# One GELU and one diagonal per expert slot, and a ring of seven buffers, in a decoder trunk with 16,384 gathered experts

## The chip, the cores and the metric

The kernel runs on one core of one Trainium2 chip. The metric is the device time of one execution in microseconds; a median of several runs is compared. The profile is of one execution, and its own time is given beside its span.

## The reference

The input x has 512 rows of 1024 float32 values. There are two layers. Each is a mixer with a residual, then an expert stage with a residual; a final RMS norm ends it. The first mixer is gated linear attention beside dilated attention, the second a gated linear recurrence. The expert stage is the same in both layers:

```
s = einsum(q, sub_keys)                       # 8 heads, two lists of 128 scores each
top_s, top_i = top_k(s, 16)
cand_s = top_s[..., 0, :, None] + top_s[..., 1, None, :]
best_s, best_c = top_k(cand_s, 16)            # 16 experts per head: 8 * 16 = 128 slots per row
g = softmax(best_s)
u, v = u_tab[ids], v_tab[ids]                 # one row of 1024 of each table per slot
act = gelu(einsum('nkd,nd->nk', u, x)) * g
out = einsum('nk,nkd->nd', act, v)
```

Every row of x thus gathers 128 expert rows of u and of v in each layer.

## The kernel before

The 512 rows are four tiles of 128 (one row per partition). With two layers that makes 8 passes, p = 0 to 7, of 128 slots, k = 0 to 127, so n = 128 p + k counts 1024 slots. Tables u and v are stored side by side, so one slot's gather brings 128 rows of 2048 float32 (8 KB each, 1 MB together) into one buffer of a ring. A slot goes through five hands:

- GpSimd (`pool`, L270) issues the gather of slot n into buffer n % BUFS once slot n - BUFS is summed (`v_done`).
- VectorE (`dot`, L287) waits until it has landed and multiplies the u half with the row of x, summing along the row: one value per partition in `hid`.
- ScalarE (`activate`, L292) applies GELU to two slots at once, pair m = slots 2m and 2m + 1, when both are dotted.
- VectorE (`place`, L302) writes for each of the two slots a 128 x 128 diagonal holding GELU value times gate. There are DIAGS = 4 diagonals; slot n reuses that of slot n - 4, so it waits for `v_done` of that slot.
- TensorE (`sum_rows`, L319) multiplies the diagonal with the v half and accumulates over the 128 slots of a pass in PSUM. The last matmul signals `v_done`, which frees the ring buffer.

The order in which VectorE does this is written by hand. In the main loop it runs `dot` of slot k, and at even k it then places the pair of slots k - 2 and k - 1. So slot 2m is placed after the dot of slot 2m + 2, two slots later. At the start of a pass the last pair of the pass before is placed after dot 0, and its sum is added to the residual (`add`, L308) after dot 2. The first ten slots (EARLY = 10) are dotted and partly placed between the steps of the first tile's choice.

Everything else is woven between the slots at fixed k. VectorE does the choice of experts for the next passes (`head`: the top 16 of two lists; `candidates`, `greatest`, `places`, `picked`, `numbers`, `gates` at the offsets STEPS behind PAIR_AT) and its part of the mixers. ScalarE does exponentials, evictions and norms. TensorE does projections in pieces, up to three behind one slot. SyncE loads the projection weights, 88 blocks of 1 MB, into two buffers. The gathers and the weights use the same 16 DMA engines.

The choice keeps its scratch in a shared region of SBUF: `topf`, `posi`, `posf`, `idf` for all heads, and `spare` (L152 to L160 write and read it in `greatest`) as a tile of its own. Each step of the choice ends in `link`, which makes VectorE wait for its own last instruction.

Of the kernel before, what the change touches and what calls it, by code (L numbers as in the profile page):

```python
# [10 lines left out]
U32 = mybir.dt.uint32  # L11
ALU = mybir.AluOpType
ACT = mybir.ActivationFunctionType
AX = mybir.AxisListType

P = 128
# [3 lines left out]
NT = T // P  # L20
# [16 lines left out]
PH, PK, NKEYS = 8, 16, 128  # L37
HK = PH * PK
# [12 lines left out]
NCAND = _at  # L51
# [33 lines left out]
ROOM = 48312  # L85


BUFS = 6
DIAGS = 4
HALF = T // 2  # L90


# [18 lines left out]
class Choice:  # L111
# [5 lines left out]
    def __init__(self, nc, s, consts, scores, room):  # L117
        self.nc, self.iota, self.scores = nc, consts["iota"], scores
        self.work = room.sb("work", [P, 2, NKEYS])
        self.cv, self.ci, self.spare = (room.sb(f"cand_{x}", [P, 2, NCAND]) for x in ("sum", "id", "left"))  # L120
        self.at = room.sb("cand_at", [P, NCAND])
        self.pick = [room.sb(f"pick{k}", [P, PK, NCAND]) for k in range(2)]
        self.top = room.sb("top", [P, 2 * PH, PK])
        self.topi = room.sb("topi", [P, 2 * PH, PK], U32)
        self.topf = room.sb("topf", [P, 2 * PH, PK])
        self.best = room.sb("best", [P, PH, PK])
        self.posi = room.sb("posi", [P, PH, PK], U32)
        self.posf = room.sb("posf", [P, PH, PK])
        self.idf = room.sb("idf", [P, HK])
        self.idi = room.sb("idi", [P, 2, HK], I32)  # L130
        self.gate = room.sb("gate", [P, 2, HK])
        self.den = room.sb("den", [P, PH])
        self.tick = room.sb("tick", [P, 1])
        self.links = 0
        self.chain, self.diff, self.exped, self.chosen, self.gated = (
            s.sem(f"choice_{x}") for x in ("chain", "diff", "exped", "chosen", "gated"))
# [31 lines left out]

    def candidates(self, dve, g):
        nc, halves = self.nc, slice(4 * g, 4 * g + 4)  # L170
        self.link(dve, nc.vector.tensor_copy(self.topf[:, halves], self.topi[:, halves]))
        tf = self.topf[:, halves].rearrange("p (h o) k -> p h o k", o=2)
        tv = self.top[:, halves].rearrange("p (h o) k -> p h o k", o=2)
        self.link(dve, nc.vector.tensor_scalar(tf[:, :, 0], tf[:, :, 0], float(NKEYS), None, ALU.mult))
        for src, dst in ((tv, self.cv), (tf, self.ci)):
            for a0, na, nb, at in CAND:
                out = dst[:, :, at:at + na * nb].rearrange("p h (a b) -> p h a b", a=na)
                one = src[:, :, 0, a0:a0 + na].unsqueeze(3).to_broadcast([P, 2, na, nb])
                two = src[:, :, 1, 0:nb].unsqueeze(2).to_broadcast([P, 2, na, nb])
                last = nc.vector.tensor_tensor(out, one, two, ALU.add)  # L180
        self.link(dve, last)

    def greatest(self, dve, g):
        heads = slice(2 * g, 2 * g + 2)
        self.best_of(dve, [(self.cv[:, k], self.spare[:, k], self.best[:, 2 * g + k], self.posi[:, 2 * g + k]) for k in range(2)])
        self.link(dve, self.nc.vector.tensor_copy(self.posf[:, heads], self.posi[:, heads]))

    def places(self, dve, g):
        at = self.at[:].unsqueeze(1).to_broadcast([P, PK, NCAND])
        for k in range(2):  # L190
            pos = self.posf[:, 2 * g + k].unsqueeze(2).to_broadcast([P, PK, NCAND])
# [3 lines left out]
    def picked(self, dve, g):  # L195
        for k in range(2):
            ids = self.ci[:, k].unsqueeze(1).to_broadcast([P, PK, NCAND])
            last = self.nc.vector.tensor_tensor(self.pick[k][:], self.pick[k][:], ids, ALU.mult)  # L198
        self.link(dve, last)

    def numbers(self, dve, p, g):

        nc = self.nc
        for k in range(2):
            h = 2 * g + k
            last = nc.vector.tensor_reduce(self.idf[:, h * PK:(h + 1) * PK], self.pick[k][:], AX.X, ALU.add)  # L206
        self.link(dve, last)
        slots, heads = slice(2 * g * PK, (2 * g + 2) * PK), slice(2 * g, 2 * g + 2)
        nc.vector.tensor_copy(self.idi[:, p % 2, slots], self.idf[:, slots]).then_inc(self.chosen, 1)
# [19 lines left out]
    def step(self, dve, p, g, at):  # L229

        if at == self.STEPS[0]:
            self.candidates(dve, g)
        if at == self.STEPS[1]:
            self.greatest(dve, g)
        if at == self.STEPS[2]:
            self.places(dve, g)
        if at == self.STEPS[3]:
            self.picked(dve, g)
        if at == self.STEPS[4]:
            self.numbers(dve, p, g)  # L240
        if at == self.STEPS[5]:
            self.gates(dve, p, g)


class Experts:
# [41 lines left out]
        self.nc.vector.tensor_tensor_reduce(out=row, in0=row, in1=self.ps[:, 6:8], scale=1.0, scalar=0.0, op0=ALU.mult, op1=ALU.add,  # L287
                                            accum_out=self.hid[:, k:k + 1]).then_inc(self.dotted, 1)

    def activate(self, act, p, m):  # L290
        act.wait_ge(self.dotted, p * HK + 2 * m + 2)
        self.nc.scalar.activation(self.act_out[:, 2 * m:2 * m + 2], self.hid[:, 2 * m:2 * m + 2], ACT.Gelu_apprx_tanh).then_inc(self.gelued, 1)  # L292

    def place(self, dve, p, m):
        dve.wait_ge(self.gelued, p * HK // 2 + m + 1)
        if m % PK == 0:
            dve.wait_ge(self.choice.gated, p * self.choice.PAIRS + m // PK + 1)
        for k in (2 * m, 2 * m + 1):
            n = p * HK + k
            if n >= DIAGS:  # L300
                dve.wait_ge(self.v_done, n - DIAGS + 1)
            self.nc.vector.tensor_scalar(self.diagonal[:, n % DIAGS], self.ident[:], self.act_out[:, k:k + 1],  # L302
                                         self.choice.gate[:, p % 2, k:k + 1], ALU.mult, ALU.mult).then_inc(self.placed, 1)

    def add(self, dve, p):
        dve.wait_ge(self.v_done, (p + 1) * HK)
# [877 lines left out]
EARLY = 10  # L1184
# [20 lines left out]
def trunk(nc, A, out):  # L1205


    with Scope(nc, "main") as s:
# [6 lines left out]
        room = Room(nc, s, ROOM)  # L1215
# [76 lines left out]
        def _(act):  # L1292
# [35 lines left out]
            for i in range(PH):  # L1328
                tail0.act_q(act, 0, i)
                if i:  # L1330
                    tail0.act_scores(act, 0, i - 1)
                if i == 3:
                    choice.exponentials(act, 0, 0)
                if i in (4, 5, 6):
                    experts.activate(act, 0, i - 4)
# [4 lines left out]
            experts.activate(act, 0, 3)  # L1340
            mix0.in_act(act, 1, 0)
            experts.activate(act, 0, 4)
# [80 lines left out]
        def _(dve):  # L1423
# [25 lines left out]
            for i in range(PH):  # L1449
                tail0.rank_dve(dve, 0, i)  # L1450
                if i % 2:
                    choice.candidates(dve, i // 2)
                    choice.greatest(dve, i // 2)
                    choice.places(dve, i // 2)
                    choice.picked(dve, i // 2)
# [86 lines left out]
            experts.place(dve, 2 * NT - 1, HK // 2 - 1)  # L1542
            experts.add(dve, 2 * NT - 1)
            final.mean_dve(dve, NT - 1)
            final.dve(dve, NT - 1)
# [170 lines left out]
```

## Time and profile before

| | |
|---|---|
| median of 3 runs | 3393.06 us (3392.06 to 3418.19) |
| the profiled execution | 3395.63 us, span 3393.8 us |
| TensorE matmul busy | 2763.0 us (81%) |
| VectorE busy | 2162.3 us (64%) |
| GpSimd busy | 983.5 us (29%) |
| ScalarE busy | 536.0 us (16%) |
| moved | 1182.28 MB, mean 348 GB/s |
| mean granted TensorE clock | 0.951 of full speed |

Times in rows are microseconds from the start of the span. "DMA share" is the mean busy share of the 16 DMA engines in a stretch; PEclk is the granted clock, 1.00 being 2.4 GHz.

### The profile page before, as it was taken

The page shows a single profiled execution, that of the slowest core. Times are in us where ns is not written, and L with a number is a line of the kernel's source. Part 1 is how long each engine was busy: PE and PEld are TensorE (multiplying, and loading weights), DVE is VectorE, ACT ScalarE, POOL GpSimd, SP SyncE. Part 2 cuts the span into 40 slices and gives each one's busy share as a digit, 9 for nine tenths or more (in the row PEclk, how much of TensorE's full clock was granted, in tenths as well). Part 3 has the DMA queues.
Part 4 walks back from the last instruction along what each step waited for, and adds up shares of the span by engine and source line. Part 5 has one row for each costly group of instructions (what it writes and reads, how often), then busy time and mean ns, then how long its engine had stood idle before and what let it go on. Part 6 is the DMA issues. An engine that isn't in the chain of part 4 may idle for free.

```text
span 3393.8 us, 33961 instructions
## 1 busy us (share of the span) xinstructions
PE 2763.0 (81%) x11992; PEld 2268.8 (67%) x11992; DVE 2162.3 (64%) x6642; ACT 536.0 (16%) x1181; POOL 983.5 (29%) x1028
## 2 busy tenths in 40 slices
PE   8989988888986877888887878878987767667776
PEld 6777776677775766767775766766776555555555
DVE  1257666675776766576677667576677656567444
ACT  3122105301111124001011105101111000001000
POOL 0002333333332233332333333332333333333332
PEclk9999999999999999999999999999999998988889
DMA  5357999999999999999999999999999999999998
GB/s 175 103 211 295 381 386 370 358 371 369 391 352 374 361 377 361 384 371 360 379 377 353 373 374 357 384 370 364 388 382 337 365 349 356 361 337 364 351 357 306
DMA packets 166634, 1182.28 MB, mean 348 GB/s; under 512 B 19376, under 2 KB 19904, under 8 KB 23872
## 3 DMA queue, kind: packets, MB, share of 16 engines
q0 software_dynamic: 147456, 1073.81, 82.5%
q1 hardware_dynamic: 19008, 106.31, 8.1%
q8 instruction: 94, 1.54, 0.2%
q14 instruction: 76, 0.62, 0.1%
HBM read 1177.95 MB, written 2.10 MB: 348 GB/s over the span
## 4 chain that ended last, share of the span: by engine, by line
DMA 44%; PE 38%; issue 9%; DVE 9%; ACT 1%; POOL 0%; SPq 0%; DVEq 0%; ACTq 0%; POOLq 0%
DMA main_ring<-in_uv,main_idi 43%; PE main_bank L319 26%; PE main_bank L355 5%; PE main_bank L353 4%; DVE main_ring L287 2%; DVE main_diagonal L302 2%; DVE main_topi L160 1%; DVE main_work L152 1%; DVE main_topi L154 0%; DVE main_hid L287 0%; PE main_bank L715 0%; DVE main_top L149 0%; DVE main_top L157 0%; DVE main_pick L198 0%; DVE main_idf L206 0%
## 5 line engine op out<-in xcount | busy, mean ns | idle before, releaser
L319 PE MATMUL main_bank<-main_ring,main_diagonal 128*128 128x256 f32 (+1 forms) x8160 | 2062.7, 404 | 596.5 <-DVE main_diagonal L302 594.4
L319 PEld LDWEIGHTS main_bank<-main_ring,main_diagonal 128*128 128x128 f32 x8160 | 1608.6, 201 | 970.1 <-DVE main_diagonal L302 711.4
L287 DVE CUSTOM_DVE_ANT_0 main_ring<-main_ring,main_bank 128x1024 f32<-128x1024 f32 x1024 | 1247.6, 1220 | 1013.6 <-DMA main_ring<-in_uv,main_idi 1003.6
L270 POOL DMA_INDIRECT main_ring<-in_uv,main_idi x1024 | 983.3, 960 | 2387.3 <-PE main_bank L319 2142.8
L292 ACT ACTIVATE main_act_out<-main_hid 128x2 f32<-128x2 f32 x512 | 104.1, 203 | 2596.0 <-DVE main_hid L287 2583.1
L355 PE MATMUL main_bank<-main_xT,main_w_block 128*128 128x256 f32 x1408 | 358.8, 384 | 4.5 <-ACT main_xT L388 4.5
L302 DVE TENSOR_SCALAR main_diagonal<-main_ident,main_act_out,main_gate 128x128 f32<-128x128 f32 x1024 | 308.8, 347 | 2.4 <-ACT main_act_out L292 2.1
L355 PEld LDWEIGHTS main_bank<-main_xT,main_w_block 128*128 128x128 f32 x1408 | 270.1, 192 | 42.5 <-ACT main_xT L388 5.0
L355 PE MATMUL main_bank<-main_xT_query,main_w_block 128*128 128x256 f32 x512 | 123.9, 383 | 0.9 <-ACT main_xT_query L388 0.9
L355 PEld LDWEIGHTS main_bank<-main_xT_query,main_w_block 128*128 128x128 f32 x512 | 98.3, 193 | 14.8 <-ACT main_xT_query L388 1.2
L292 ACT ACT_TABLE_LOAD x80 | 102.6, 1283 | 1.4
L353 PE MATMUL main_bank<-main_w_block,main_xT 128*128 128x256 f32 x384 | 93.5, 382 | 0.0
L287 DVE DVE_READ_ACCUMULATOR2_ANT main_hid<- 128x1 f32 x1024 | 84.8, 83 | 0.0
L353 PEld LDWEIGHTS main_bank<-main_w_block,main_xT 128*128 128x128 f32 x384 | 72.4, 191 | 10.5 <-issue 0.9
L353 PE MATMUL main_bank<-main_w_block,main_a_gate 128*128 128x256 f32 x256 | 67.4, 387 | 0.0
L353 PE MATMUL main_bank<-main_w_block,main_mixT 128*128 128x256 f32 x256 | 62.8, 387 | 0.7 <-ACT main_mixT L826 0.7
L198 DVE TENSOR_TENSOR main_pick<-main_pick,main_cand_id 128x800 f32<-128x800 f32 x64 | 60.5, 986 | 0.6
L192 DVE TENSOR_TENSOR main_pick<-main_posf,main_cand_at 128x800 f32<-128x800 f32 x64 | 60.4, 986 | 0.2
L206 DVE TENSOR_REDUCE main_idf<-main_pick 128x16 f32<-128x800 f32 x64 | 60.0, 979 | 0.2
L353 PEld LDWEIGHTS main_bank<-main_w_block,main_a_gate 128*128 128x128 f32 x256 | 50.2, 196 | 7.4
L353 PEld LDWEIGHTS main_bank<-main_w_block,main_mixT 128*128 128x128 f32 x256 | 49.6, 195 | 7.9 <-ACT main_mixT L826 0.9
L143 DVE MEMSET main_tick<- 128x1 f32 x704 | 41.5, 59 | 2.2
(188 smaller groups left out, 1183.5 us busy)
## 6 DMA issues: line engine op xcount, KB each, us to landing
main_w_block<-in_w_query SPq DMA_DIRECT2D x32, 1024.0 KB
main_w_block<-in_w_ab SPq DMA_DIRECT2D x24, 1024.0 KB
main_ring<-in_uv,main_idi POOLq DMA_INDIRECT x1024
main_w_block<-in_w_c_in SPq DMA_DIRECT2D x16, 1024.0 KB
main_w_block<-in_w_out SPq DMA_DIRECT2D x8, 1024.0 KB
main_w_block<-in_w_c_out SPq DMA_DIRECT2D x8, 1024.0 KB
main_att_bias<-in_att_bias SPq DMA_DIRECT2D x16, 256.0 KB
main_resid<-in_x SPq DMA_DIRECT2D x2, 1024.0 KB, 7.6
```

Source lines behind the costliest of these rows:

```text
L143: self.nc.vector.memset(self.tick[:], 0.0)
L152: last = nc.vector.match_replace(copy, best[:, low], values, NEG)
L192: last = self.nc.vector.tensor_tensor(self.pick[k][:], pos, at, ALU.is_equal)
L198: last = self.nc.vector.tensor_tensor(self.pick[k][:], self.pick[k][:], ids, ALU.mult)
L206: last = nc.vector.tensor_reduce(self.idf[:, h * PK:(h + 1) * PK], self.pick[k][:], AX.X, ALU.add)
L270: nc.gpsimd.indirect_dma_start(self.ring[n % self.bufs], None, self.uv[p // NT], bass.IndirectOffsetOnAxis(self.choice.idi[:, p % 2, k:k + ...
L287: self.nc.vector.tensor_tensor_reduce(out=row, in0=row, in1=self.ps[:, 6:8], scale=1.0, scalar=0.0, op0=ALU.mult, op1=ALU.add, accum_out=s ...
L292: self.nc.scalar.activation(self.act_out[:, 2 * m:2 * m + 2], self.hid[:, 2 * m:2 * m + 2], ACT.Gelu_apprx_tanh).then_inc(self.gelued, 1)
L302: self.nc.vector.tensor_scalar(self.diagonal[:, n % DIAGS], self.ident[:], self.act_out[:, k:k + 1], self.choice.gate[:, p % 2, k:k + 1], ...
L319: last = self.nc.tensor.matmul(self.ps[:, 4 + at // T, at % T:at % T + wide], self.diagonal[:, n % DIAGS], self.ring[n % self.bufs][:, D + ...
L353: last = nc.tensor.matmul(out, xT[:, d, cols], w[:, d], start=d == 0, stop=d == KD - 1)
L355: last = nc.tensor.matmul(out, w[:, d, cols], xT[:, d], start=d == 0, stop=d == KD - 1)
```

## The change

GELU and diagonal are made for each slot by itself: `activate` and `place` take a slot k and not a pair. Slot k is activated as soon as it is dotted and placed right behind the dot of slot k + 1, whether k is even or odd. The residual add moves from behind dot 2 to behind dot 1 of the next pass. The ring has seven buffers in place of six, and three diagonals in place of four. To make room in SBUF, the scratch of the choice is kept for one pair of heads (`topf`, `posi`, `posf`, `idf`), and `topf` and `spare` lie on top of the `pick` tiles, which are written after they are read.

```diff
-BUFS = 6
-DIAGS = 4
+BUFS = 7
+DIAGS = 3
...
-        self.cv, self.ci, self.spare = (room.sb(f"cand_{x}", [P, 2, NCAND]) for x in ("sum", "id", "left"))
+        self.cv, self.ci = (room.sb(f"cand_{x}", [P, 2, NCAND]) for x in ("sum", "id"))
         self.at = room.sb("cand_at", [P, NCAND])
+        at_pick = room.next
         self.pick = [room.sb(f"pick{k}", [P, PK, NCAND]) for k in range(2)]
+        self.topf = room.part("topf", at_pick, [P, 4, PK])
+        self.spare = room.part("cand_left", at_pick + PK * NCAND, [P, 2, NCAND])
...
-        self.posi = room.sb("posi", [P, PH, PK], U32)
-        self.posf = room.sb("posf", [P, PH, PK])
-        self.idf = room.sb("idf", [P, HK])
+        self.posi = room.sb("posi", [P, 2, PK], U32)
+        self.posf = room.sb("posf", [P, 2, PK])
+        self.idf = room.sb("idf", [P, 2 * PK])
...
-    def activate(self, act, p, m):
-        act.wait_ge(self.dotted, p * HK + 2 * m + 2)
-        self.nc.scalar.activation(self.act_out[:, 2 * m:2 * m + 2], self.hid[:, 2 * m:2 * m + 2], ...)
-
-    def place(self, dve, p, m):
-        dve.wait_ge(self.gelued, p * HK // 2 + m + 1)
-        ...
-        for k in (2 * m, 2 * m + 1):
-            n = p * HK + k
-            if n >= DIAGS:
-                dve.wait_ge(self.v_done, n - DIAGS + 1)
-            self.nc.vector.tensor_scalar(self.diagonal[:, n % DIAGS], ...).then_inc(self.placed, 1)
+    def activate(self, act, p, k):
+        act.wait_ge(self.dotted, p * HK + k + 1)
+        self.nc.scalar.activation(self.act_out[:, k:k + 1], self.hid[:, k:k + 1], ...)
+
+    def place(self, dve, p, k):
+        n = p * HK + k
+        dve.wait_ge(self.gelued, n + 1)
+        ...
+        if n >= DIAGS:
+            dve.wait_ge(self.v_done, n - DIAGS + 1)
+        self.nc.vector.tensor_scalar(self.diagonal[:, n % DIAGS], ...).then_inc(self.placed, 1)
...
                 for k in range(0 if p else EARLY, HK):
-                    if k % 2:
-                        experts.activate(act, p, k // 2)
+                    experts.activate(act, p, k)
...
-                if i in (3, 4, 5, 6):
-                    experts.place(dve, 0, i - 3)
+                if i >= 3:
+                    experts.place(dve, 0, 2 * i - 6)
+                    experts.place(dve, 0, 2 * i - 5)
...
                     experts.dot(dve, p, k)
-                    if p and k == 2:
+                    if p and k == 1:
                         experts.add(dve, p - 1)
-                    if k % 2 == 0 and k:
-                        experts.place(dve, p, k // 2 - 1)
-                    elif k == 0:
-                        experts.place(dve, p - 1, HK // 2 - 1)
+                    if k == 0:
+                        experts.place(dve, p - 1, HK - 1)
+                    elif p or k > EARLY:
+                        experts.place(dve, p, k - 1)
```

## Rows read from the trace of the kernel before

**Rows 1.** The page, DMA share and rate in 40 slices of the span

```profile
DMA  5357999999999999999999999999999999999998
GB/s 175 103 211 295 381 386 370 358 371 369 391 352 374 361 377 361 384 371 360 379 377 353 373 374 357 384 370 364 388 382 337 365 349 356 361 337 364 351 357 306
```

**Rows 2.** The page, gather queue (share of 16 engines), and the chain

```profile
q0 software_dynamic: 147456, 1073.81, 82.5%
...
DMA 44%; PE 38%; issue 9%; DVE 9%; ACT 1%; POOL 0%; SPq 0%; DVEq 0%; ACTq 0%; POOLq 0%
```

**Rows 3.** Busy time by stretch: engines, PEclk, DMA share, GB/s

```profile
264.00:325.00 61.00, 59.88 (x272) 49.65 (x273) 43.76 (x180) 13.84 (x24) 13.16 (x14) 1.00 0.77 293
...
2600.00:3375.00 775.00, 546.51 (x2087) 431.67 (x2086) 467.07 (x1242) 51.84 (x160) 251.15 (x262) 0.91 0.94 356
...
325.00:3375.00 3050.00, 2461.98 (x10531) 2020.32 (x10530) 2019.90 (x6022) 444.65 (x992) 960.50 (x1000) 0.95 0.95 367
```

**Rows 4.** Four of the 123 windows of 25 us between 300 and 3375

```profile
300.00:325.00 25.00, 24.10 (x109) 20.04 (x108) 17.68 (x59) 8.43 (x13) 7.64 (x9) 1.00 1.00 398
...
3275.00:3300.00 25.00, 19.26 (x68) 15.50 (x67) 13.14 (x26) 0.94 (x5) 7.33 (x8) 0.80 0.93 348
...
3325.00:3350.00 25.00, 18.83 (x74) 14.64 (x73) 13.70 (x28) 0.81 (x4) 8.49 (x10) 0.92 0.99 386
3350.00:3375.00 25.00, 16.01 (x67) 12.68 (x66) 12.95 (x25) 0.81 (x4) 7.49 (x8) 0.96 0.97 363
```

**Rows 5.** Timeline of one undisturbed pair: start, us, engine, line, what

```profile
2912.65 1.22 DVE L287 CUSTOM_DVE_ANT_0 main_ring<-main_ring,main_bank 128x1024 f32<-128x1024 f32 x1 [1.86 <-DMA main_ring<-in_uv,main_idi]
...
2915.09 1.22 DVE L287 CUSTOM_DVE_ANT_0 main_ring<-main_ring,main_bank 128x1024 f32<-128x1024 f32 x1 [0.60 <-DMA main_ring<-in_uv,main_idi]
...
2917.75 1.22 DVE L287 CUSTOM_DVE_ANT_0 main_ring<-main_ring,main_bank 128x1024 f32<-128x1024 f32 x1 [1.44 <-DMA main_ring<-in_uv,main_idi]
...
2918.90 0.60 DVE L302 TENSOR_SCALAR main_diagonal<-main_ident,main_act_out,main_gate 128x128 f32<-128x128 f32 x2
...
2919.29 3.72 PE L319 MATMUL main_bank<-main_ring,main_diagonal 128*128 128x256 f32 x16 [1.38 <-DVE main_diagonal L302]
...
2921.56 0.94 POOL L270 DMA_INDIRECT main_ring<-in_uv,main_idi  x1 [2.44 <-PE main_bank L319]
...
2923.29 0.94 POOL L270 DMA_INDIRECT main_ring<-in_uv,main_idi  x1 [0.79 <-PE main_bank L319]
```

**Rows 6.** Timeline around a long wait of GpSimd

```profile
2893.25 0.94 POOL L270 DMA_INDIRECT main_ring<-in_uv,main_idi  x1 [0.79 <-PE main_bank L319]
...
2900.88 0.94 POOL L270 DMA_INDIRECT main_ring<-in_uv,main_idi  x1 [6.69 <-PE main_bank L319]
...
2906.47 1.22 DVE L287 CUSTOM_DVE_ANT_0 main_ring<-main_ring,main_bank 128x1024 f32<-128x1024 f32 x1 [2.99 <-DMA main_ring<-in_uv,main_idi]
```

**Rows 7.** Busy time in 0.7 us of that stretch

```profile
2901.80:2902.50 0.70, 0.70 (x4) 0.58 (x3) 0.25 (x1) 0.00 (x0) 0.02 (x1) 0.74 0.00 0
```

**Rows 8.** The page, costliest groups: busy, mean ns, idle before

```profile
L319 PE MATMUL main_bank<-main_ring,main_diagonal 128*128 128x256 f32 (+1 forms) x8160 | 2062.7, 404 | 596.5 <-DVE main_diagonal L302 594.4
...
L287 DVE CUSTOM_DVE_ANT_0 main_ring<-main_ring,main_bank 128x1024 f32<-128x1024 f32 x1024 | 1247.6, 1220 | 1013.6 <-DMA main_ring<-in_uv,main_idi 1003.6
...
L292 ACT ACTIVATE main_act_out<-main_hid 128x2 f32<-128x2 f32 x512 | 104.1, 203 | 2596.0 <-DVE main_hid L287 2583.1
...
L302 DVE TENSOR_SCALAR main_diagonal<-main_ident,main_act_out,main_gate 128x128 f32<-128x128 f32 x1024 | 308.8, 347 | 2.4 <-ACT main_act_out L292 2.1
...
L198 DVE TENSOR_TENSOR main_pick<-main_pick,main_cand_id 128x800 f32<-128x800 f32 x64 | 60.5, 986 | 0.6
```

**Rows 9.** Timeline of the start: placing slots 6, 7, and two sums

```profile
268.63 0.60 DVE L302 TENSOR_SCALAR main_diagonal<-main_ident,main_act_out,main_gate 128x128 f32<-128x128 f32 x2
...
278.14 1.89 PE L319 MATMUL main_bank<-main_ring,main_diagonal 128*128 128x256 f32 x8
...
293.88 1.99 PE L319 MATMUL main_bank<-main_ring,main_diagonal 128*128 128x256 f32 x8
```

More of the change, by code:

```diff
@@ L170, in candidates @@
         nc, halves = self.nc, slice(4 * g, 4 * g + 4)
-        self.link(dve, nc.vector.tensor_copy(self.topf[:, halves], self.topi[:, halves]))
-        tf = self.topf[:, halves].rearrange("p (h o) k -> p h o k", o=2)
+        self.link(dve, nc.vector.tensor_copy(self.topf[:], self.topi[:, halves]))
+        tf = self.topf[:].rearrange("p (h o) k -> p h o k", o=2)
         tv = self.top[:, halves].rearrange("p (h o) k -> p h o k", o=2)
@@ L183, in greatest, with places, picked @@
     def greatest(self, dve, g):
[L184 to L188, printed above, removed]
+        self.best_of(dve, [(self.cv[:, k], self.spare[:, k], self.best[:, 2 * g + k], self.posi[:, k]) for k in range(2)])
+        self.link(dve, self.nc.vector.tensor_copy(self.posf[:], self.posi[:]))
+    def places(self, dve):
         at = self.at[:].unsqueeze(1).to_broadcast([P, PK, NCAND])
         for k in range(2):
-            pos = self.posf[:, 2 * g + k].unsqueeze(2).to_broadcast([P, PK, NCAND])
+            pos = self.posf[:, k].unsqueeze(2).to_broadcast([P, PK, NCAND])
             last = self.nc.vector.tensor_tensor(self.pick[k][:], pos, at, ALU.is_equal)
         self.link(dve, last)
-    def picked(self, dve, g):
+    def picked(self, dve):
         for k in range(2):
@@ L204, in numbers @@
         for k in range(2):
-            h = 2 * g + k
-            last = nc.vector.tensor_reduce(self.idf[:, h * PK:(h + 1) * PK], self.pick[k][:], AX.X, ALU.add)
+            last = nc.vector.tensor_reduce(self.idf[:, k * PK:(k + 1) * PK], self.pick[k][:], AX.X, ALU.add)
         self.link(dve, last)
         slots, heads = slice(2 * g * PK, (2 * g + 2) * PK), slice(2 * g, 2 * g + 2)
-        nc.vector.tensor_copy(self.idi[:, p % 2, slots], self.idf[:, slots]).then_inc(self.chosen, 1)
+        nc.vector.tensor_copy(self.idi[:, p % 2, slots], self.idf[:]).then_inc(self.chosen, 1)
         first = self.best[:, heads, 0:1].to_broadcast([P, 2, PK - 1])
@@ L235, in step @@
         if at == self.STEPS[2]:
-            self.places(dve, g)
+            self.places(dve)
         if at == self.STEPS[3]:
-            self.picked(dve, g)
+            self.picked(dve)
         if at == self.STEPS[4]:
@@ L288, in dot @@
                                             accum_out=self.hid[:, k:k + 1]).then_inc(self.dotted, 1)
-    def activate(self, act, p, m):
-        act.wait_ge(self.dotted, p * HK + 2 * m + 2)
-        self.nc.scalar.activation(self.act_out[:, 2 * m:2 * m + 2], self.hid[:, 2 * m:2 * m + 2], ACT.Gelu_apprx_tanh).then_inc(self.gelued, 1)
-    def place(self, dve, p, m):
-        dve.wait_ge(self.gelued, p * HK // 2 + m + 1)
-        if m % PK == 0:
-            dve.wait_ge(self.choice.gated, p * self.choice.PAIRS + m // PK + 1)
-        for k in (2 * m, 2 * m + 1):
-            n = p * HK + k
-            if n >= DIAGS:
-                dve.wait_ge(self.v_done, n - DIAGS + 1)
-            self.nc.vector.tensor_scalar(self.diagonal[:, n % DIAGS], self.ident[:], self.act_out[:, k:k + 1],
-                                         self.choice.gate[:, p % 2, k:k + 1], ALU.mult, ALU.mult).then_inc(self.placed, 1)
+    def activate(self, act, p, k):
+        act.wait_ge(self.dotted, p * HK + k + 1)
+        self.nc.scalar.activation(self.act_out[:, k:k + 1], self.hid[:, k:k + 1], ACT.Gelu_apprx_tanh).then_inc(self.gelued, 1)
+    def place(self, dve, p, k):
+        n = p * HK + k
+        dve.wait_ge(self.gelued, n + 1)
+        if k % (2 * PK) == 0:
+            dve.wait_ge(self.choice.gated, p * self.choice.PAIRS + k // (2 * PK) + 1)
+        if n >= DIAGS:
+            dve.wait_ge(self.v_done, n - DIAGS + 1)
+        self.nc.vector.tensor_scalar(self.diagonal[:, n % DIAGS], self.ident[:], self.act_out[:, k:k + 1],
+                                     self.choice.gate[:, p % 2, k:k + 1], ALU.mult, ALU.mult).then_inc(self.placed, 1)
     def add(self, dve, p):
@@ L1334, in _ @@
                 if i in (4, 5, 6):
-                    experts.activate(act, 0, i - 4)
+                    experts.activate(act, 0, 2 * i - 8)
+                    experts.activate(act, 0, 2 * i - 7)
             tail0.act_scores(act, 0, PH - 1)
@@ L1339, in _ @@
             choice.exponentials(act, 0, 2)
-            experts.activate(act, 0, 3)
+            experts.activate(act, 0, 6)
+            experts.activate(act, 0, 7)
             mix0.in_act(act, 1, 0)
-            experts.activate(act, 0, 4)
+            experts.activate(act, 0, 8)
+            experts.activate(act, 0, 9)
             mix0.in_act(act, 1, 1)
@@ L1453, in _ @@
                     choice.greatest(dve, i // 2)
-                    choice.places(dve, i // 2)
-                    choice.picked(dve, i // 2)
+                    choice.places(dve)
+                    choice.picked(dve)
                     choice.numbers(dve, 0, i // 2)
@@ L1541, in _ @@
                             final.dve(dve, k // 10 - 1)
-            experts.place(dve, 2 * NT - 1, HK // 2 - 1)
+            experts.place(dve, 2 * NT - 1, HK - 1)
             experts.add(dve, 2 * NT - 1)
```

1 line of the change is left out of this document (removed).

## The prediction

> **What bounds the kernel now.** I read the page's slices first. From the fifth slice on the 16 DMA engines are busy nine tenths of the time or more, at 337 to 391 GB/s [rows 1]. The queue table says what they carry: 1073.81 MB of the 1182 MB are the 1024 gathers, and these alone take 82.5% of 16 engines over the span [rows 2]. The chain gives DMA its largest share, 44%, with TensorE next at 38% [rows 2]. On VectorE the wait before the dots is for landings, 1003.6 us, while the place instruction waits 2.4 us in all [rows 8]. So the gathers are the bound, and the question is how much of the DMA engines' time is lost between them.
>
> The windows by stretch answer that. Between 325 and 3375 us, 3050 us with exactly 1000 gathers issued, the DMA share is 0.95 and the rate 367 GB/s; in the last 775 us of it, where no weights are loaded beside the gathers, 0.94 and 356 GB/s [rows 3]. I then cut 300 to 3375 us into 123 windows of 25 us and sorted them by DMA share. In 30 of them (first and last in rows 4: 300 and 3325 us) it is 0.99 or more, and they average 393 GB/s. In 27 it is 0.97 or 0.98 and they average 374 (the last: 363 at 3350 us). In 31 it is 0.94 to 0.96, average 360; in 26 it is 0.90 to 0.93, average 351 (348 at 3275 us); in 9 less, average 330 [rows 4]. The same traffic goes 7% faster when the engines never run dry. The rate falls more than the share does, so the transfers after a gap are slower too.
>
> Why they run dry is seen in the timeline. One undisturbed pair: slot 2m is dotted at 2912.65, slot 2m + 1 at 2915.09, slot 2m + 2 at 2917.75, and only then, at 2918.90, are the first two placed; TensorE sums both from 2919.29, 3.72 us; GpSimd may refill their buffers at 2921.56 and 2923.29 [rows 5]. The two buffers are thus held 8.9 and 8.2 us from dot to refill. With six buffers and 2.7 us from dot to dot, a buffer comes round in 16.2 us, so about 7.3 and 8.0 us are left from issue to dot. A transfer issued with nothing ahead of it takes 2906.47 - 2900.88 = 5.6 us to its dot [rows 6]. About 2 us of slack is less than two steps of the choice cost VectorE (two instructions of 986 ns each for one of them [rows 8]) or a slow sum. When it is gone we see what stands at 2893.25: no gather is issued for 6.69 us because TensorE hasn't freed a buffer, and at 2901.8 to 2902.5 the DMA share is 0.00 [rows 6, 7].
>
> **The change part by part.**
>
> **Placing slot by slot.** Slot 2m of rows 5 would be placed after the dot of 2915.09 and its read of the sum, at about 2916.3; after a place the refill comes 2921.56 - 2918.90 = 2.66 us later. That is 2919.0, a hold of 6.3 us in place of 8.9. Slot 2m + 1 is placed at 2918.9 as now but is no longer summed behind its neighbour: refill at 2921.6, a hold of 6.5 in place of 8.2. Mean gain 2.15 us of lead for every transfer.
>
> **The seventh buffer.** It adds one slot period, 2.7 us, to the round. Together a buffer comes round in 18.9 us, is held 6.4, and leaves 12.5 us from issue to dot against the 5.6 that a lone transfer needs. Slack goes from 2 to about 7 us. The one dry stretch I followed came after a delay of 6.69 us, of which some 2 us is an ordinary wait [rows 5, 6]; so most would be covered.
>
> **What that is worth.** 3050 us at 367 GB/s is 1119 MB [rows 3]. The weights must be moved too, so no traffic is saved; only the rate rises. I take three quarters of the time at the rate of the full windows and one quarter at that of the next class, because VectorE's and TensorE's busy stretches will still bite: 0.75 x 393 + 0.25 x 374 = 388 GB/s [rows 4]. 1119 MB at 388 is 2884 us, a gain of 166 us. The ends for the range: all at 398, the rate of a good full window, is 2812 us, gain 238; all at 374 is 2992 us, gain 58.
>
> **Is there room on the engines?** TensorE is busy 2462 us in the 3050, 2.46 us per slot at a clock of 0.95 [rows 3]; at 2.88 us per slot it is at 85%. VectorE has 2020 us, 70% of the new 2884. Its own cost grows: two diagonals back to back take 0.60 us, one takes 0.347, so 512 x 0.09 = 46 us more busy, all under the wait for landings (1003.6 us, of which 166 go) [rows 5, 8]. If that cover were gone it would be 46 us. ScalarE runs 512 more GELUs at 203 ns, 104 us on an engine that waits 2583 us for dots [rows 8]. Their distance to the place stays one dot: GELU of slot k must end before dot k + 1 does, 1.22 us, in place of the same for the odd slot of a pair. Behind a ScalarE job at odd k the next GELU is now due one slot earlier. What is queued behind a late place on VectorE is the next dot, which has slack. Zero; bounds: 10 us lost from the 2.1 us seen now [rows 8], nothing gained.
>
> **Three diagonals.** VectorE's place of slot n now waits for the sum of slot n - 3; behind that wait stand the next dots and the choice. In the main loop slot n - 3 was placed three slots (8 us) earlier and its sum takes 1.86 us plus up to three product pieces, so it is zero there; at most a few us in all. At the start it shows. Slots 6 and 7 are placed at 268.63; slot 7 must now wait for the sum of slot 4, which TensorE starts at 278.14 and ends at 280.03 [rows 9]. VectorE stands for about 11 us. The dots 8 and 9 and the last step of the choice follow, some 16 us, so slots 8 and 9 are placed near 296.5, where TensorE, which is busy 59.88 of these 61 us [rows 3], wanted slot 8 at 293.88 [rows 9]. Cost 2.6 us; bounds 0 and 11.
>
> **The add behind dot 1**: it waits for the sum of the pass's last slot, placed one dot before; in the worst case about 1 us in each of 7 passes, otherwise under the wait for the landing. **The end**: the last sum is of one slot and not of two, 1.9 us less [rows 5]. **The folded scratch**: same instructions, same shapes, on one engine in the same order with its own waits between them: zero. Its SyncE queue and the weights' transfers are not moved.
>
> Sum: 3393.8 - 166 + 2.6 + 1 - 1.9 = 3229.5 us of span. The profiled execution's time is 1.8 us over its span and 2.6 us over the median of the runs, so the median to expect is 3228.7; I say 3228.
>
> **The rivals.**
>
> **The limit moves to the engines' order (half the gain or less).** The slack is eaten by VectorE stretches in which heads and choice steps come together, or by TensorE where three pieces lie behind a slot. Then the whole lies in the class of 374 GB/s: gain 58 us, 3337. For it: windows where VectorE is near full exist, and in the 61 us at the start TensorE is at 98% [rows 3]. Against: 28 of the 30 full windows lie before 2600 us, where this work is, and they average 394.
>
> **The memory is the limit.** If 367 GB/s were what this core gets from memory over long stretches, deeper prefetch would only lengthen each transfer, DMA share would rise to 1.00 and the rate would stay: 3394 less 2, about 3392. Against: 30 windows at 393, and slices of 391 and 388 over 85 us [rows 1, 4].
>
> The Trainium skill (DMA: Bandwidth & Descriptors, section Specifications) gives about 358 GB/s as the memory limit of one core, with 368 in the vendor's cost model. By the first the 1119 MB would take 3126 us, longer than today, by the second 3041; the windows above 390 disagree with both.
>
> **Slower: TensorE's clock.** The sums now come one by one with a gap of about 1 us after each, not in pairs. If the granted clock fell to its lower level of 1.2 GHz more often for that, TensorE would become the bound: its 2.46 us per slot at 0.95 are 2.34 at full clock, and they reach today's 3.05 us per slot when the mean granted clock is 0.77. From there on it is slower; at 0.74 it is 3160 us for the 1000 slots, 3505 in all. For it: where TensorE does only sums the clock is already 0.91, against 0.95 over the whole [rows 3], and it stood at 0.74 in the dry stretch [rows 7]. Against: these low spots followed the longer gaps of the pairs, and with faster gathers TensorE's busy share in that stretch rises from 70% to about 77%.
>
> The change does what it says in the code read here; that the seventh buffer brings nothing is the rival of the memory limit.
>
> **How the numbers follow.** The forecast, 3228, has 0.77; half the gain or less, 3337, 0.12; memory, 3392, 0.06; slower, 3505, 0.05. The range goes from 3165 (398 GB/s, 3157, nearly reached) to 3340, which takes in the first rival's value. About 1% is what a measurement of this kernel can tell from no change, 34 us. Faster by more than that is the forecast and nearly all of the first rival, 0.88; within 1% 0.07; slower 0.05.
>
> **What would show each step.** Right: DMA share from 325 us to the last gather 0.98 to 1.00 at 385 GB/s or more; GpSimd's waits for TensorE of the 6.69 us kind gone, and refills 2.7 us behind each place; VectorE's wait for landings near 840 us; one idle of about 11 us before the diagonal L302 at 269 us; TensorE's clock no lower than 0.95. Wrong: a share near 1.00 at a rate still near 370 (the memory); VectorE waiting in L302 for TensorE in the main loop (the diagonals); waits for ScalarE at L302 well over 10 us; a mean clock under 0.85.

## The result and the profile after

The changed kernel takes 3028.31 us (median of 4 runs, 3025.63 to 3031.74) against 3395.41 us of the kernel before in the same session: a ratio of 0.8901, 95% interval 0.8869 to 0.8933. The forecast was 3228 with a range down to 3165. The direction was right and the gain more than twice as large.

The page of the changed kernel, its slices and the gather queue, answers to [rows 1, 2]:

```profile
DMA  5246999999999999999999999999999999999997
GB/s 189 94 175 239 414 412 424 383 422 426 426 405 410 408 426 418 415 426 423 426 410 412 412 427 419 409 427 416 427 419 391 421 426 418 426 418 406 425 423 332
...
q0 software_dynamic: 147456, 1073.81, 85.6%
...
PE 53%; DMA 27%; DVE 10%; issue 7%; ACT 1%; POOL 0%; DVEq 0%; SPq 0%; ACTq 0%; POOLq 0%
```

The bytes are the same. From the fifth slice to the last but one they move at 383 to 427 GB/s, where before the best slice had 391 (the last slice, with the end of the work in it, has 332; before 306). By stretch (engines, PEclk, DMA share, GB/s), the answer to [rows 3]; the third row holds the same 1000 gathers as the 3050 us of before:

```profile
264.00:325.00 61.00, 58.74 (x262) 48.92 (x261) 38.14 (x162) 12.39 (x24) 12.69 (x14) 0.97 0.70 262
...
2300.00:3008.00 708.00, 561.59 (x2304) 421.06 (x2303) 511.18 (x1428) 87.41 (x319) 271.49 (x280) 0.99 1.01 419
325.00:3008.00 2683.00, 2377.47 (x10543) 1942.51 (x10542) 2016.31 (x6028) 544.43 (x1495) 967.40 (x1000) 0.98 1.01 417
```

So 367 us went between 325 us and the last gathers. Two things changed there. The DMA share rose from 0.95 to 1.01 (it passes 1 where packets overlap: the traces have stretches with 17 packets under way on 16 engines). And the rate within that share rose too: 367 / 0.95 = 386 GB/s before, 417 / 1.01 = 413 now. Windows of 25 us, where [rows 4] show 398 in a full one:

```profile
725.00:750.00 25.00, 20.32 (x90) 15.78 (x88) 17.02 (x43) 6.28 (x17) 8.55 (x10) 1.00 1.01 428
2050.00:2075.00 25.00, 25.00 (x119) 22.03 (x118) 21.32 (x52) 4.62 (x12) 9.51 (x10) 1.00 1.01 421
2600.00:2625.00 25.00, 20.42 (x82) 14.81 (x83) 14.90 (x30) 2.03 (x10) 10.13 (x11) 1.00 1.01 426
```

Of the 108 windows from 300 to 3000 us, 56 have 426 to 428 GB/s. That is a flat top. Of the 123 windows of the kernel before one came near it, and the next best has 405:

```profile
1025.00:1050.00 25.00, 12.40 (x46) 9.69 (x46) 14.28 (x63) 0.61 (x3) 5.62 (x6) 0.91 1.01 420
```

The timeline of one slot, the answer to [rows 5]:

```profile
2600.86 1.22 DVE L287 CUSTOM_DVE_ANT_0 main_ring<-main_ring,main_bank 128x1024 f32<-128x1024 f32 x1 [0.95 <-DMA main_ring<-in_uv,main_idi]
...
2603.31 1.22 DVE L287 CUSTOM_DVE_ANT_0 main_ring<-main_ring,main_bank 128x1024 f32<-128x1024 f32 x1 [0.96 <-DMA main_ring<-in_uv,main_idi]
...
2604.45 0.34 DVE L301 TENSOR_SCALAR main_diagonal<-main_ident,main_act_out,main_gate 128x128 f32<-128x128 f32 x1
...
2604.85 1.59 PEld L318 LDWEIGHTS main_bank<-main_ring,main_diagonal 128*128 128x128 f32 x8 [0.86 <-DVE main_diagonal L301]
2604.85 1.99 PE L318 MATMUL main_bank<-main_ring,main_diagonal 128*128 128x256 f32 x8 [0.46 <-DVE main_diagonal L301]
...
2607.12 0.96 POOL L270 DMA_INDIRECT main_ring<-in_uv,main_idi  x1 [1.51 <-PE main_bank L318]
```

A slot is dotted at 2600.86, placed at 2604.45 behind the dot of the next, and its buffer is refilled at 2607.12: a hold of 6.26 us, with a refill 2.67 us behind the place. The prediction had 6.3 and 2.66. The period of this slot is 2.45 us (2603.31 - 2600.86); over the whole stretch it is 2.68 us (2683 us for 1000 gathers), where the kernel before has 3.05.

The costliest groups, as in [rows 8], with VectorE's wait for landings down from 1003.6 to 623.8 us:

```profile
L287 DVE CUSTOM_DVE_ANT_0 main_ring<-main_ring,main_bank 128x1024 f32<-128x1024 f32 x1024 | 1247.7, 1219 | 634.8 <-DMA main_ring<-in_uv,main_idi 623.8
...
L292 ACT ACTIVATE main_act_out<-main_hid 128x1 f32<-128x1 f32 x1024 | 206.9, 203 | 2201.9 <-DVE main_hid L287 2200.9
L301 DVE TENSOR_SCALAR main_diagonal<-main_ident,main_act_out,main_gate 128x128 f32<-128x128 f32 x1024 | 358.3, 350 | 33.1 <-PE main_bank L318 17.2
```

And the start, as in [rows 9]:

```profile
276.33 1.70 PEld L318 LDWEIGHTS main_bank<-main_ring,main_diagonal 128*128 128x128 f32 x8
...
278.54 0.35 DVE L301 TENSOR_SCALAR main_diagonal<-main_ident,main_act_out,main_gate 128x128 f32<-128x128 f32 x1 [12.63 <-PE main_bank L318]
```

VectorE stands 12.63 us for the sum of slot 4, as foreseen (11 us).

### The profile page after: what moved, and what is told of

Its sections match the earlier page's. It is cut to its first block, busy times and chain, and to the rows that moved or that the text cites. A ratio compares the mean times of both kernels' runs of the same rounds, so it can differ in the third digit from the quotient of the medians.

```text
span 3026.6 us, 34984 instructions
## 1 busy us (share of the span) xinstructions
PE 2675.8 (88%) x11992; PEld 2188.5 (72%) x11992; DVE 2157.1 (71%) x6642; ACT 637.1 (21%) x1693; POOL 990.8 (33%) x1028
## 4 chain that ended last, share of the span: by engine, by line
PE 53%; DMA 27%; DVE 10%; issue 7%; ACT 1%; POOL 0%; DVEq 0%; SPq 0%; ACTq 0%; POOLq 0%
PE main_bank L318 36%; DMA main_ring<-in_uv,main_idi 27%; PE main_bank L354 9%; PE main_bank L352 5%; DVE main_diagonal L301 2%; DVE main_ring L287 1%; PE main_bank L714 1%; DVE main_pick L199 1%; DVE main_hid L287 1%; DVE main_topi L162 1%; DVE main_work L154 1%; PE main_bank L522 1%; DVE main_pick L193 1%; DVE main_topi L156 1%; PE main_bank L730 1%
## 5 line engine op out<-in xcount | busy, mean ns | idle before, releaser
L318 PE MATMUL main_bank<-main_ring,main_diagonal 128*128 128x256 f32 (+1 forms) x8160 | 1996.0, 391 | 315.7 <-DVE main_diagonal L301 314.6
L318 PEld LDWEIGHTS main_bank<-main_ring,main_diagonal 128*128 128x128 f32 x8160 | 1536.1, 193 | 685.6 <-DVE main_diagonal L301 463.7
L287 DVE CUSTOM_DVE_ANT_0 main_ring<-main_ring,main_bank 128x1024 f32<-128x1024 f32 x1024 | 1247.7, 1219 | 634.8 <-DMA main_ring<-in_uv,main_idi 623.8
L292 ACT ACTIVATE main_act_out<-main_hid 128x1 f32<-128x1 f32 x1024 | 206.9, 203 | 2201.9 <-DVE main_hid L287 2200.9
L301 DVE TENSOR_SCALAR main_diagonal<-main_ident,main_act_out,main_gate 128x128 f32<-128x128 f32 x1024 | 358.3, 350 | 33.1 <-PE main_bank L318 17.2
L920 DVE CUSTOM_DVE_ANT_0 main_att_s<-main_bank,main_att_bias 128x128 f32<-128x128 f32 (+3 forms) x32 | 15.6, 487 | 39.1 <-PE main_bank L714 38.2
```

The source lines that it names most:

```text
L292: self.nc.scalar.activation(self.act_out[:, k:k + 1], self.hid[:, k:k + 1], ACT.Gelu_apprx_tanh).then_inc(self.gelued, 1)
L318: last = self.nc.tensor.matmul(self.ps[:, 4 + at // T, at % T:at % T + wide], self.diagonal[:, n % DIAGS], self.ring[n % self.bufs][:, D + ...
```

## The experiments

Ratios are to the kernel before on the same chip. Theory A says that the lead from issue to dot sets the rate, however it is gained; B that placing evenly does it; C is the prediction's own: lead counts until the engines never run dry, and the rate is then 393 GB/s.

**The two parts alone, and less than the kernel before.** Pairs with seven buffers:

```diff
 # kernel before
-BUFS = 6
-DIAGS = 4
+BUFS = 7
+DIAGS = 3
 # and class Choice of the changed kernel
```

> The kernel before with seven buffers, three diagonals and the folded scratch, GELU and diagonals still in pairs. Theory A (lead time): only the lead from issue to dot counts, buffers times the slot period less the hold; here 7 x 2.7 - 8.5 = 10.4 us against 7.5 before and 12.5 after, so the time lies over half way from 3395 to 3028: about 3150 us. Theory B (evenness): the refills come two together, so the queue still runs short before each pair of issues; placing slot by slot brings most of the gain: about 3280 us here. Theory C (my prediction): lead counts only until the engines never run dry, and then the rate is 393 GB/s: never under 3200 us.

Measured 3078.79 us, ratio 0.9052 (0.9004 to 0.9100).

```diff
 # changed kernel
-BUFS = 7
+BUFS = 6
```

> The changed kernel with six buffers in place of seven. Theory A: lead 6 x 2.7 - 6.4 = 9.8 us, a little less than with pairs and seven buffers: about 3180 us. Theory B: about 3080 us, clearly faster than pairs with seven buffers. Theory C: not under 3200 us.

Measured 3109.61 us, ratio 0.9148 (0.9092 to 0.9204).

```diff
 # changed kernel
-BUFS = 7
+BUFS = 5
```

> The changed kernel with five buffers. Theory A: lead 5 x 2.7 - 6.4 = 7.1 us, a little less than the 7.5 of the kernel before: about 3400 us, like the kernel before or slower. Theory B: faster than the kernel before, about 3250 us.

Measured 3472.16 us, ratio 1.0221 (1.0164 to 1.0277).

The windows of the three, in this order, from 325 us to the last gathers:

```profile
325.00:3056.00 2731.00, 2370.03 (x10553) 1979.55 (x10552) 2018.04 (x6035) 446.36 (x994) 964.01 (x1001) 0.98 1.00 410
```

```profile
325.00:3085.00 2760.00, 2393.89 (x10550) 1936.18 (x10549) 2021.92 (x6038) 544.25 (x1495) 971.59 (x1001) 0.99 0.99 406
```

```profile
325.00:3427.00 3102.00, 2488.94 (x10579) 1978.68 (x10579) 2037.83 (x6064) 547.36 (x1501) 965.31 (x1005) 0.97 0.94 362
```

The order is that of the lead. With the prediction's own working (buffers x 2.7 less the hold): 7.1 us of lead 3472, 7.7 before 3395 to 3408 (6 x 2.7 - 8.5; the expectations have 7.5), 9.8 us 3110, 10.4 us 3079, 12.5 us 3028. The means from issue to dot in the traces lie closer together, in the same order: 7.9, 8.3, 9.2, 9.3 and 11.1 us. Counted from the start of an issue to the last packet of its gather, 2.1, 2.2, 2.7, 2.7 and 3.1 gathers are in flight on average. B falls: slot by slot with six buffers isn't faster than pairs with seven, and with five it is some 2% slower than pairs with six. C falls: two of the three are far under 3200. Either half of the change alone brings most of the gain: 9.5% for the buffer, 8.5% for placing by slot, 11% for both (each of these runs has the folded scratch and three diagonals as well, and with them the ring's address, below). Most of the step lies between 7.7 and 9.8 us of reckoned lead; theory A's even spacing was too simple, and put the first two runs 70 us too high and the third 72 us too low.

**How many gathers may be in flight.** To take the queue by itself, all else as changed, GpSimd also waits for an older landing (D = 4, 3, 2):

```diff
 # changed kernel, Experts.pool
                 if n >= self.bufs:
                     pool.wait_ge(self.v_done, n - self.bufs + 1)
+                if n >= D:
+                    pool.wait_ge(self.landed[(n - D) % self.bufs], 16 * ((n - D) // self.bufs + 1))
```

> The changed kernel, in which GpSimd issues the gather of slot n only when that of slot n - 4 has landed: at most four in flight, all else as it is. Theory A (the length of the queue sets how fast the bytes move): in the changed kernel three or four are mostly in flight, so little changes: 3030 to 3060 us. Theory D (the rate came from something else in the change, for instance TensorE's and VectorE's steadier rhythm): 3028 us, and the caps of three and two change little as well until the engines run dry.

Measured 3029.48 us, ratio 0.8886 (0.8861 to 0.8911).

> The same with at most three in flight. The issue follows a landing by over 0.3 us, lasts 0.94 us and the first bytes move about 1.6 us after its start, so for two of each 2.5 us only two are really queued. Theory A: between the kernel before and the changed one, 3100 to 3200 us, at a rate of 390 to 405 GB/s. Theory D: under 3060 us.

Measured 3320.80 us, ratio 0.9730 (0.9701 to 0.9759).

> The same with at most two in flight. A lone transfer takes 5.6 us from issue to dot, so two at a time give at best one per 2.8 us, and theory A, with each transfer slowed by the short queue as well, says one per 3.2 us or more: 3500 to 3800 us, slower than the kernel before although no buffer is short. Theory D: one per 2.8 to 3.0 us, 3200 to 3350 us.

Measured 3692.28 us, ratio 1.0823 (1.0792 to 1.0854).

Their windows, D = 4, 3, 2:

```profile
325.00:3007.00 2682.00, 2377.45 (x10548) 1938.96 (x10547) 2099.52 (x6032) 544.16 (x1495) 953.12 (x1000) 0.99 1.01 418
```

```profile
325.00:3312.00 2987.00, 2480.72 (x10567) 1978.37 (x10565) 2140.52 (x6051) 544.92 (x1496) 945.60 (x1002) 0.96 0.98 375
```

```profile
325.00:3675.00 3350.00, 2563.60 (x10550) 1990.27 (x10549) 2157.42 (x6032) 544.69 (x1496) 941.89 (x1002) 0.95 0.89 334
```

What matters are the last two columns, share and rate. With D = 3 the engines are busy 0.98 of the time, more than the 0.95 of the kernel before, and yet move 375 GB/s: 383 per full share, against 414 with D = 4. The transfers themselves are slower in a short queue. Theory D is out: only the issue was changed. VectorE's diagonals take longer too, but with D = 4 nearly as much as with D = 3 (451 and 500 ns, last section), and D = 4 costs nothing.

The packets in the traces show where the rate goes. In each of these kernels and in the kernel before, most of the 8 KB packets (73 to 97%) take 309 ns, which on 16 engines is 424 GB/s. The means differ: 315 ns in the changed kernel and with D = 4, 341 with D = 3 and in the kernel before, 349 with D = 2. On 16 engines these are 416, 385 and 375 GB/s, the rates per full share again. In the kernel before 7.5% of the packets take over 400 ns, in the changed one 1.5%. Packets that started while fewer than 12 were under way took 563 ns on average in the stretch from 325 to 3375 us of the kernel before, but they hold only 17% of the time lost over 309 ns; 63% is lost by packets that started while 15 or more were. So a queue that is short costs without any gap that the share would show. Why those packets are slow stays open: the trace doesn't say which engine carries a packet, nor whether that one had just run dry. The cap of three cost more than A had said (3321 against 3100 to 3200). On average 2.2 gathers are in flight with D = 3, as in the kernel before, 2.8 with D = 4 and 1.6 with D = 2. The timeline with D = 3 shows why three allowed are two at work:

```profile
2909.04 1.22 DVE L289 CUSTOM_DVE_ANT_0 main_ring<-main_ring,main_bank 128x1024 f32<-128x1024 f32 x1 [0.71 <-DMA main_ring<-in_uv,main_idi]
2909.78 0.94 POOL L272 DMA_INDIRECT main_ring<-in_uv,main_idi  x1 [1.50 <-DMA main_ring<-in_uv,main_idi]
...
2911.45 1.22 DVE L289 CUSTOM_DVE_ANT_0 main_ring<-main_ring,main_bank 128x1024 f32<-128x1024 f32 x1 [0.69 <-DMA main_ring<-in_uv,main_idi]
2912.19 0.94 POOL L272 DMA_INDIRECT main_ring<-in_uv,main_idi  x1 [1.48 <-DMA main_ring<-in_uv,main_idi]
```

The issue starts 0.73 us behind the start of the dot and lasts 0.94 us; by its end two thirds of the 2.41 us period are over, and in that time only two gathers stand in the queue.

**The address of the ring.** Four diagonals needed room, so the one-word tile of the links was moved:

```diff
 # changed kernel
-DIAGS = 3
+DIAGS = 4
-        self.tick = room.sb("tick", [P, 1])
+        self.tick = s.sb("tick", [P, 1])
```

> The changed kernel with four diagonals (the one-word tile that the links write moves out of the shared region, which makes the room). The wait of 12.6 us of VectorE at the start is gone; the prediction's cost of the third diagonal was 2.6 us, so 3022 to 3027 us against 3028; if VectorE's other waits on TensorE cost something too, up to 10 us faster.

Measured 3063.60 us, ratio 0.8985 (0.8964 to 0.9006): about 1% slower than the changed kernel, and no theory had it. The tile stood ahead of the ring, so the ring had moved by 32 bytes as well. The next three part the two:

```diff
 # before_aligned: kernel before; after_misaligned: changed kernel
-        self.tick = room.sb("tick", [P, 1])
+        self.tick = s.sb("tick", [P, 1])
 # diags_4_aligned: changed kernel, that and
-DIAGS = 3
+DIAGS = 4
-        self.den = room.sb("den", [P, PH])
+        self.den = s.sb("den", [P, PH])
```

> The kernel before with the one-word tile of the links moved out of the shared region. Only addresses change: the ring then begins at a multiple of 64 bytes (169472) and not 32 bytes past one (169504). Theory E (alignment): packets into a ring 32 bytes off take 0.311 to 0.320 us and not 0.309; the folded scratch happened to move the ring onto a multiple of 64, which is 1 to 1.5% of the transfer time and a part of the gain that no step of the prediction has. This kernel is then 0.8 to 1.3% faster than before, 3355 to 3375 us. Theory F (the four diagonals made diags_4b slow, not the address): no difference.

Measured 3400.31 us, ratio 0.9978 (0.9950 to 1.0006).

> The changed kernel, three diagonals, with the same tile moved out: the ring begins 32 bytes past a multiple of 64 (166880), as in diags_4b. Theory E: 3058 to 3068 us, like diags_4b, with the DMA share at 1.01 and a lower rate. Theory F: 3028 us.

Measured 3067.71 us, ratio 0.9001 (0.8966 to 0.9036).

> The changed kernel with four diagonals and two small tiles moved out, so that the ring begins at a multiple of 64 bytes (166848, which is an odd multiple of 64). Theory E: 3020 to 3028 us, the fourth diagonal ending VectorE's wait at the start. Theory F: 3060 us or more.

Measured 3056.85 us, ratio 0.8972 (0.8936 to 0.9008). Three diagonals with the ring moved by 32 bytes are as slow as four, so the address matters; but a multiple of 64 didn't mend it. Against multiples of 256 bytes these rings lie as follows: 166880 is 224 past one, 166848 is 192 past one, 169472 is one, and the ring of the kernel before, 169504, is 32 past one. So after_misaligned doesn't stand where the kernel before does, though both are 32 bytes past a multiple of 64. The next four part it further:

```diff
 # diags_4_512: changed kernel
-DIAGS = 3
+DIAGS = 4
-        self.hid = room.sb("hid", [P, HK])
+        self.hid = s.sb("hid", [P, HK])
 # after_plus_128 (32 words) and after_plus_256 (64 words): changed kernel
+        room.next += 32
         ring = room.sb("ring", [P, BUFS, 2 * D])
```

> The changed kernel once more, on the chip of the next three: 3028 us, and its ratio to the kernel before is what the others are held against.

Measured 3030.54 us, ratio 0.8902 (0.8877 to 0.8926).

> Four diagonals, the ring where the changed kernel has it (166912, a multiple of 512 bytes); the tile of dot results moved out of the shared region to make the room. Theory E (only the ring's address made the two kernels with four diagonals slow): 3020 to 3028 us, VectorE's wait at the start gone. Theory F (the fourth diagonal costs): 3055 us or more. Both in part: between.

Measured 3030.76 us, ratio 0.8893 (0.8868 to 0.8919).

> Three diagonals, the ring 128 bytes further on (167040, an odd multiple of 128). Theory E with a wish for 64 or 128 bytes: 3028 us. Theory E with a wish for 256 or more: 3045 to 3065 us, the packets at 0.311 to 0.320 us as in the others. Theory F: 3028 us.

Measured 3058.86 us, ratio 0.8983 (0.8959 to 0.9008).

> Three diagonals, the ring 256 bytes further on (167168, an odd multiple of 256). If the ring wants a multiple of 512 bytes, 3045 to 3065 us; otherwise 3028 us.

Measured 3028.34 us, ratio 0.8897 (0.8873 to 0.8922).

The same 490 us of pure slots in after_again, after_plus_128 and after_plus_256:

```profile
2500.00:2990.00 490.00, 382.98 (x1554) 281.95 (x1553) 340.90 (x893) 59.37 (x219) 186.70 (x195) 1.00 1.01 421
```

```profile
2540.00:3030.00 490.00, 379.44 (x1531) 278.80 (x1529) 336.87 (x884) 58.75 (x216) 186.14 (x193) 0.99 1.01 415
```

```profile
2500.00:2990.00 490.00, 384.04 (x1557) 282.90 (x1556) 340.94 (x896) 59.37 (x219) 187.55 (x195) 1.00 1.01 423
```

At one DMA share of 1.01 the rate is 421 and 423 GB/s with the ring at a multiple of 256 bytes, 415 with it at an odd multiple of 128. The fourth diagonal costs nothing. The tiles behind the ring move with it, but the difference shows in the transfers, at the same share.

The folded scratch had put the ring from 169504 (32 bytes past a multiple of 256) onto 166912, a multiple, by chance. Had it ended 128 to 224 bytes past one, 28 to 40 us of the gain would be missing. How much of the gain the move from 169504 brought is another question, and it is little as far as the runs show: before_aligned makes the same move in the kernel before, for 0.2%, within an interval from 0.5% faster to none. Nor is it the short queue that hides the cost there. Of the packets that started with three gathers in flight, those that take 310 to 329 ns (not 309) are 13% in the kernel before and 78% in after_misaligned, against 3% in before_aligned and under 1% in the changed kernel. The changed kernel with its ring 32 bytes past a multiple of 256 wasn't run.

**The start.**

```diff
 # changed kernel, the steps of the first choice
-                if i >= 3:
-                    experts.place(dve, 0, 2 * i - 6)
-                    experts.place(dve, 0, 2 * i - 5)
+                for k in {3: (0, 1), 4: (2, 3), 5: (4, 5), 6: (6,), 7: (7, 8, 9)}.get(i, ()):
+                    experts.place(dve, 0, k)
```

> The changed kernel with slot 7 placed one step of the start later, together with slots 8 and 9, so that VectorE doesn't stand for the sum of slot 4. The prediction priced that stand at 2.6 us: 3025 to 3027 us; if TensorE never waited for it, 3028 us; if the whole 12.6 us were on the path, 3016 us.

Measured 3023.12 us (3019.49 to 3026.63, 6 runs), ratio 0.8871 (0.8836 to 0.8906). It is the fastest version run, 5 to 7 us under the changed kernel (3028.31, and 3030.54 when run again), though they were on different chips and the intervals of the ratios overlap. It can't be the stand of VectorE alone: diags_4_512 ends that too and shows no gain. This stays open.

## Why the prediction was right or wrong

**What bounds the kernel: right.** The gathers did, and dry engines were one cause. Its first reading leaves out the last slice of [rows 1], which has 306 GB/s at a share of eight tenths; nothing hangs on it.

**The lead: right in kind.** In the slot read above the hold is 6.26 us against 6.3 forecast, and the refill comes 2.67 behind the place against 2.66. GpSimd's idle times of over 6 us before a gather fell from 28 to 1 (from 325 us on), and the DMA share is full. In size it gained less than reckoned: the mean from issue to dot rose from 8.3 to 11.1 us, not from 7.65 to 12.5. The period of 2.7 us was read from two neighbouring dots; the mean of the kernel before was 3.05. Taken alone, the share explains about half: 1119 MB at 386 GB/s per share and a share of 1.01 (390 GB/s) are 2869 us, 181 us less than 3050.

**"What that is worth" is the step that failed: the rate.** It took the mean of the full windows, 393 GB/s, for the rate of engines that are never dry (388 with a quarter at 374), and called 398, the end of its range, the rate of a good full window, though its own windows went up to 420. Those windows were full by share, but in a kernel with 2.2 gathers in flight on average. Measured were 417 GB/s over the stretch. The cap runs show the rate per full share at 375 with two allowed (334 / 0.89), 383 with three, 414 with four. The kernel before stands at 386. This second half, 2869 less 2683 = 186 us, was in no term. The prediction had seen the sign of it ("the rate falls more than the share does, so the transfers after a gap are slower too") and laid it to the gaps. That was part of it: 17% of the time that slow packets lost in the kernel before fell to those that started with fewer than 12 under way. The rest was lost between the gaps, with most engines at work, as the D = 3 run shows too (share 0.98, 375 GB/s). The trace of before held the ceiling already, in its packets of 309 ns (424 GB/s on 16 engines).

**The folded scratch: zero** held as far as the runs show, but in part by luck: the folding also moved the ring, which the prediction didn't consider. The old place, 32 bytes past a multiple of 256, costs at most 0.5% in the kernel before; other places would have cost the changed kernel 28 to 40 us. That it came out at a multiple of 256 was chance.

**The costs beside it** held. The stand at the start is 12.63 us (11 forecast); what of it is on the path isn't settled: start_order is 5 to 7 us faster and diags_4_512, which ends the stand too, isn't. VectorE's waits for TensorE at L301 are 17.2 us in 5 cases, 12.6 of them that one. VectorE's wait for ScalarE there is 15.4 us in 7 cases, over the bound of 10; VectorE still waits 623.8 us for landings, so it is probably hidden, which no run shows. VectorE's busy time at L301 rose by 358.3 - 308.8 = 49.5 us (46 forecast). The small waits of the adds and the end weren't measured by themselves. The granted clock rose from 0.951 to 0.981, so the rival of the clock was wrong in sign.

**The rivals.** A limit in the engines' order (374 GB/s) didn't come: TensorE is at 89% of the stretch and its work is now 53% of the chain, so it is the next to bind, but the DMA share stays 1.01. The memory rival is refuted: 417 GB/s over 2683 us. The Trainium skill (DMA: Bandwidth & Descriptors, section Specifications) gives 358 GB/s as the memory's limit for one core, which these runs exceed, and 435 GB/s as the ceiling of the fabric, which the flat top of 426 to 428 comes close to, 2% below it.

## What to carry to other kernels

When a ring of buffers feeds the bound, count the lead (buffers times period less the hold) and the transfers in flight (here four had to be allowed, about three on average), and don't go by the share of the DMA engines alone: at 0.95 and at 0.98 there was still a tenth to gain. A hold can be shortened as well as a ring lengthened, and here either alone gave most of it. Don't take the mean of the full windows of a kernel with a short queue for the ceiling of one with a long queue; the usual time of one packet, 309 ns, gave the better ceiling. Start the ring at a multiple of 256 bytes, and check that it is still there when a tile ahead of it changes.

## What the runs showed of the hardware

- Rate against gathers of 1 MB allowed in flight in the changed kernel: two 334 GB/s, three 375, four 418, and no more with the seven buffers alone as the limit (417). The mean time of an 8 KB packet was 349, 341, 315 and 315 ns, with 309 for most packets in each.
- The start of the ring in a partition, gathers of 8 KB rows, changed kernel: a multiple of 256 bytes gave 3028 to 3031 us (166912 and 167168), 128 past one 3059, 192 past 3057, 224 past 3064 and 3068. In the kernel before, 32 past one cost 0.2% against a multiple (none to 0.5%). The Trainium skill (DMA: Bandwidth & Descriptors, section How a descriptor splits into AXI transactions) says of reads that a transaction starts at a multiple of 256 bytes and that the bytes before a descriptor's start are fetched too and cost beats of 32 bytes. By that rule, as an estimate, 8 KB cost 256 beats at a multiple of 256, 257 at 32 past, 260 at 128, 262 at 192 and 263 at 224. The packets of under 330 ns average 309.1 to 309.2 ns at a multiple, 310.1 at 32 past, 312.3 at 128, 312.8 at 192 and 313.6 at 224: the order agrees, the rise is half to two thirds of the rule's. That the rule holds for the write into SBUF, which is what was moved here, the section doesn't say.
- VectorE's diagonal takes 576 ns in place of 344 (medians) when it begins 0.4 to 0.5 us after the start of a GpSimd issue: over 500 ns in 99% of 681 such cases with D = 3. When it begins earlier in the issue, or 0.6 us or more after its start, it takes 344 ns as it does alone. In the changed kernel only 24 diagonals begin at that point; with a cap the issue and the dot both follow a landing, so that most do (the issue of 2909.78 above, the place at 2910.19). These are the groups of the changed kernel, of D = 4 and of D = 3:

```profile
L301 DVE TENSOR_SCALAR main_diagonal<-main_ident,main_act_out,main_gate 128x128 f32<-128x128 f32 x1024 | 358.3, 350 | 33.1 <-PE main_bank L318 17.2 <-ACT main_act_out L292 15.4
```

```profile
L303 DVE TENSOR_SCALAR main_diagonal<-main_ident,main_act_out,main_gate 128x128 f32<-128x128 f32 x1024 | 461.4, 451 | 30.6 <-ACT main_act_out L294 16.8 <-PE main_bank L320 13.2
```

```profile
L303 DVE TENSOR_SCALAR main_diagonal<-main_ident,main_act_out,main_gate 128x128 f32<-128x128 f32 x1024 | 511.3, 500 | 28.7 <-PE main_bank L320 15.3 <-ACT main_act_out L294 13.1
```
